# Order of two steps in an RWKV-7 recurrence: sums of squares and features ahead of the state's products and update

## The chip, the cores and the metric

One core of a Trainium2 chip. The metric is the device time of one execution in microseconds (us), the median of several executions. The profile is one further execution taken by the hardware profiler.

## The reference, cut to what matters

The kernel computes a stack of transformer blocks on 256 tokens of width 1024. The change lies in one part of it, the bidirectional RWKV-7 time mixing. For each direction and each of 16 heads of width 64 the reference runs

```
state = state * w_t + (state @ a_t) outer b_t + v_t outer k_t
y_t   = state @ r_t
```

over the tokens (`a_t` is -kk, `b_t` is kk times the learning rate), forward and backward, followed by a group norm, a bonus term and a gate. Everything after it (attention, mixtures of experts, MLPs) is untouched.

## The kernel before

The recurrence works on 8 chunks. A chunk here is a pair of heads (128 channels on the partitions) over all 256 tokens and both directions z. The tokens are two blocks of 128; the state S0 carries the first block's result to the second. Within a chunk the triangular systems are solved by five levels of products: TensorE makes W (`level_w`, L937), ScalarE copies it to `Wb`, TensorE makes the two products XY (`level_xy`, L950 and L955), and VectorE adds them (`level`).

The work is a software pipeline written out by hand. One loop `for s in range(-2, C + 2)` stands on each of TensorE (`pe`), ScalarE (`act`), VectorE (`dve`) and, in a shorter form, GpSimd (`pool`). In pass s the engines work on chunk e = s+2 (norms and decay inputs), f = s+1 (features), c = s (levels), p = s-1 (solve with the state) and g = s-2 (group norm, gate), each only where the number lies in 0..7 (`on_e`, `on_f`, `on_c`, `on_p`, `on_g`). Every engine goes through its list in order; semaphores (`ev(...)`) tie them together.

Steps that the text names:
- features of chunk f on VectorE: four products of 512 columns giving `ar`, `bt`, `kt`; at the end `rw_feat` is raised (L2334). GpSimd, TensorE and ScalarE (its square for e) wait on it.
- sums of squares sm0, sm1 of chunk f on TensorE: 64 products of 64x64 from `ar` and `bt` (L1060). ScalarE copies half of each to `Ast`, VectorE multiplies the other half by a mask (`x0`) and then gives the bank back (L2349).
- S, the state's increment, on TensorE (L1032), and the update of S0 on VectorE (four small products, L2072).
- Z1, products of `ar` with S0 on TensorE (L1047), added to `Zv` by VectorE.
- P1, R1, U1: the solve of the second token block (L964, L974, L984).
- BK, transposes of `bt` and `kt` (L1076); rb (L1086); kk (L1092), the norms' sums of chunk e; var (L1065), the variance of chunk g.
- `ada_blocks(1)`: a step on VectorE of 128x2048 elements that belongs to the adaptive-norm products of another part and is woven into the recurrence. It reads a ring tile loaded by DMA.

All these results of TensorE lie in PSUM. The group "rw" has four banks. `RW_SLOT` lists all tiles in the order in which a pass claims them; `RWN` numbers them through all passes, and tile number m uses bank m mod 4. `claim` lets TensorE wait until tile m-4 has been given back:

```
def claim(g, m, it=None, per=0):
    ...
    elif m >= n:
        pe.wait_ge(free(g, m), m // n)
    return tile(g, m)
```

Of the kernel before, what the change touches and what calls it, by code (L numbers as in the profile page):

```python
# [27 lines left out]
P = 128  # L28
S = 256
# [271 lines left out]
def _plan(name, lo, hi=0, align=False, flip=0, out=0):  # L301
# [8 lines left out]

RW_SLOT = (("P0", 1), ("mean", 2), ("R0", 1), ("U0", 1), ("Zv", 0), ("S", 1), ("V", -1), ("Z1", 1), ("sm0", -1), ("sm1", -1),
           ("var", 2), ("P1", 1), ("BK", -1), ("R1", 1), ("rb0", -1), ("rb1", -1), ("kk", -2), ("U1", 1), ("wa0", -2), ("wa1", -2),
           ("n60", -1), ("n61", -1), ("y", 1), ("bn", -1), ("g", 2), ("ka0", -1), ("ka1", -1), ("kr0", -1), ("kr1", -1))
RWN = {}
# [132 lines left out]
def build(nc, d, out_d):  # L449
    ctx = ExitStack()  # L450
    with ctx:
# [100 lines left out]
        ar = [work(1024).rearrange("p (i n) -> p i n", i=2) for _ in range(3)]  # L552
# [6 lines left out]
        Zv = [work(512) for _ in range(2)]  # L559
# [4 lines left out]
        S0 = work(256).rearrange("p (z n) -> p z n", z=2)  # L564
        ys, sq = work(512), work(512)
        fac = [work(2) for _ in range(3)]
        HALF = (slice(0, 64), slice(64, 128))
# [11 lines left out]
        def ev(name):  # L579
            if name not in named:  # L580
                named[name] = sem(name)
            return named[name]
# [225 lines left out]
        def _(pe):  # L808
            mm = nc.tensor.matmul
# [104 lines left out]
            def rwkv():  # L914
# [3 lines left out]
                def cl(k, i):  # L918
                    return claim("rw", RWN[k, i])

                def fin(ins):
                    ins.then_inc(tile_ready["rw"], 1)

                def gone(k, i):
                    pe.wait_ge(free("rw", RWN[k, i]), RWN[k, i] // 4 + 1)
# [62 lines left out]
                for s in range(-2, C + 2):  # L988
                    e, f, c, p, g = s + 2, s + 1, s, s - 1, s - 2
                    on_e, on_f, on_c, on_p, on_g = e < C, 0 <= f < C, 0 <= c < C, 0 <= p < C, 0 <= g < C  # L990
# [20 lines left out]
                    if on_c:  # L1011
# [3 lines left out]
                        t = cl("Zv", c)  # L1015
                        for z in (0, 1):
                            for j in (0, 1):
                                for h in (0, 1):
                                    a = z * 256 + j * P + 64 * h
                                    last = mm(t[:, a:a + 64], Aak[:, h, z, j, :], Vt[c % 3][:, j, 64 * h:64 * h + 64], start=True, stop=True)  # L1020
# [3 lines left out]
                    if on_p:  # L1024
                        gone("U0", p)
                        gone("BK", p)
                        t = cl("S", p)
                        for z in (0, 1):
                            for i in (0, 1):
                                for h in (0, 1):  # L1030
                                    r = HALF[h]
                                    last = mm(t[r, 64 * z:64 * z + 64], BK[p % 2][:, z, i, r], Vt[p % 3][:, z, r] if i else Uu[:, 0, z, r],  # L1032
                                              start=i == 0, stop=i == 1, skip_group_check=True)
                        fin(last)
                    if on_f:
                        t = cl("V", f)
                        for j in range(2):
                            last = nc.tensor.transpose(t[:, j * P:(j + 1) * P], vT[:, f, j * P:(j + 1) * P], ident)
                        fin(last)
                    if on_c:  # L1040
                        level_w(c, 3)
                    if on_p:
                        gone("S", p)
                        t = cl("Z1", p)
                        for z in (0, 1):
                            a = z * 256 + (1 - z) * P
                            last = mm(t[:, z * P:z * P + P], ar[p % 3][:, 0, a:a + P], S0[:, z, :], start=True, stop=True)  # L1047
                        fin(last)
                    if on_f:
                        pe.wait_ge(ev("rw_feat"), f + 1)  # L1050
                        t = [cl(f"sm{h}", f) for h in (0, 1)]
                        for i in (0, 1):
                            for z in (0, 1):
                                for j in (0, 1):
                                    for b in (0, 1):
                                        a = slice(z * 256 + j * P + 64 * b, z * 256 + j * P + 64 * b + 64)
                                        o = 256 * i + (2 * z + j) * 64
                                        for h in (0, 1):
                                            x_, y_ = ar[f % 3][HALF[h], 0, a], bt[HALF[h], a]
                                            last = mm(t[h][HALF[b], o:o + 64], y_ if i else x_, x_ if i else y_, start=True, stop=True)  # L1060
                                            if (i, z, j, b) == (1, 1, 1, 1):
                                                fin(last)
                    if on_g:
                        pe.wait_ge(ev("rw_sq"), g + 1)
                        fin(mm(cl("var", g), blk64, sq, start=True, stop=True))  # L1065
# [5 lines left out]
                    if on_f:  # L1071
                        t = cl("BK", f)
                        for z in (0, 1):
                            for i in (0, 1):
                                a = z * 256 + z * P
                                last = nc.tensor.transpose(t[:, (2 * z + i) * P:(2 * z + i + 1) * P], (kt if i else bt)[:, a:a + P], ident)  # L1076
# [5 lines left out]
                    if on_f:  # L1082
                        t = [cl(f"rb{h}", f) for h in (0, 1)]
                        for q in range(4):
                            for h in (0, 1):
                                last = mm(t[h][:, q * P:(q + 1) * P], bt[HALF[h], q * P:(q + 1) * P], ar[f % 3][HALF[h], 1, q * P:(q + 1) * P],  # L1086
                                          start=True, stop=True)
# [9 lines left out]
                    if on_e:  # L1097
                        for z in (0, 1):
                            t = cl(f"wa{z}", e)
                            for i in range(2):  # L1100
                                last = mm(t[:, i * S:(i + 1) * S], lora2[HALF[z], i * D + e * P:i * D + (e + 1) * P], th[HALF[z], i, :],
                                          start=True, stop=True)
                            fin(last)
                    if on_f:
                        t = [cl(f"n6{h}", f) for h in (0, 1)]
                        for z in (0, 1):
                            for j in (0, 1):
                                a = z * 256 + j * P
                                for h in (0, 1):
                                    last = mm(t[h][HALF[z], 64 * j:64 * j + 64], bt[HALF[h], a + 64 * z:a + 64 * z + 64],  # L1110
                                              ar[f % 3][HALF[h], 0, a + 64 - 64 * z:a + 128 - 64 * z], start=True, stop=True)
# [4 lines left out]
                    if on_p:  # L1116
# [3 lines left out]
                        t = cl("y", p)  # L1120
                        for z in (0, 1):
                            for ji in (0, 1):
                                j = z if ji == 0 else 1 - z
                                a = z * 256 + j * P
# [6 lines left out]
                                for h, r in enumerate(HALF):  # L1131
                                    last = mm(t[r, a:a + P], Vt[p % 3][:, j, r], Ark[p % 2][:, h, z, j, :], start=False, stop=True,
                                              skip_group_check=True)
# [4 lines left out]
                    if on_g:  # L1138
                        t = cl("g", g)
                        for z in (0, 1):  # L1140
                            last = mm(t[:, z * S:z * S + S], lora2[:, (2 + z) * D + g * P:(2 + z) * D + (g + 1) * P], th[:, 2 + z, :],
                                      start=True, stop=True)
# [3 lines left out]
                    if on_f:  # L1146
                        for i, k in ((0, "ka"), (1, "kr")):
                            t = [cl(f"{k}{h}", f) for h in (0, 1)]
                            for q in range(4):
                                for h in (0, 1):  # L1150
                                    last = mm(t[h][:, q * P:(q + 1) * P], kt[HALF[h], q * P:(q + 1) * P],
                                              ar[f % 3][HALF[h], i, q * P:(q + 1) * P], start=True, stop=True)
# [904 lines left out]
        def _(dve):  # L2057
            chain, own = sem("dve_chain"), [0]
            v = nc.vector
            MUL, ADD, SUB = ALU.mult, ALU.add, ALU.subtract  # L2060
# [10 lines left out]
            def ts(out, a, s1, s2, o1, o2=ALU.bypass):  # L2071
                return v.tensor_scalar(out, a, s1, s2, o1, o2)  # L2072
# [177 lines left out]
            def rwkv():  # L2250
# [3 lines left out]
                def got(k, i):  # L2254
                    ready(dve, "rw", RWN[k, i])
                    return tile("rw", RWN[k, i])

                def let(ins, k, i):
                    ins.then_inc(free("rw", RWN[k, i]), 1)
# [25 lines left out]
                for s in range(-2, C + 2):  # L2285
                    e, f, c, p, g = s + 2, s + 1, s, s - 1, s - 2
                    on_e, on_f, on_c, on_p, on_g = e < C, 0 <= f < C, 0 <= c < C, 0 <= p < C, 0 <= g < C
                    if s == -1:
                        modulation("ada1")
                    if on_f:  # L2290
# [4 lines left out]
                        for j in range(2):  # L2295
                            o, i_ = (a[:, S:2 * S][:, j * P:(j + 1) * P] for a in (cum, ea))
                            last = v.tensor_tensor_scan(o[:, ::-1], ones, i_[:, ::-1], 0.0, MUL, SUB)
# [19 lines left out]
                        K(stt(two(cum), both(kkx), float(2 ** 20), two(ea[:, 512:1024]), MUL, MUL))  # L2317
                    if on_c:
                        level(c, 2)
                    if on_p:  # L2320
                        t = got("S", p)
                        for z in (0, 1):
                            for r in HALF:
                                last = ts(S0[r, z, r], t[r, 64 * z:64 * z + 64], fac[p % 3][r, z:z + 1], None, MUL)
                        let(last, "S", p)
                    if on_f:
                        dve.wait_ge(ev("rw_E"), f + 1)
                        a_ = ar[f % 3]
# [2 lines left out]
                    if on_f:  # L2331
                        tt(bt, cum, e3, MUL)
                        K(tt(kt, km, e3, MUL))
                        dve.sem_inc(ev("rw_feat"), 1)  # L2334
                    if on_p:
                        a = Zv[p % 2][:, P:3 * P]
                        let(tt(a, got("Z1", p)[:, 0:S], a, ADD), "Z1", p)
                        ada_blocks(1)
                    if on_c:
                        level(c, 3)  # L2340
                    if on_f:
                        x0 = rmask("x0").rearrange("p (z t) -> p z t", z=2)[:, :, None, :].to_broadcast([P, 2, 2, 64])
                        X = XY[f % 3][:, :, 0, :]
                        for h in (0, 1):
                            dve.wait_ge(ev("rw_A"), 2 * f + h + 1)
                            t = got(f"sm{h}", f)[:, 256:512].rearrange("p (z j t) -> p z j t", z=2, j=2)
                            last = tt(X[:, :, h * P:(h + 1) * P].rearrange("p z (j t) -> p z j t", j=2), t, x0, MUL)
# [622 lines left out]
```

## Time and profile before

| | us |
|---|---|
| median of 3 runs | 3048.99 |
| lowest, highest | 3048.26, 3053.26 |
| profiled execution, its own time | 3056.66 |
| its span (first to last instruction) | 3054.9 |

The span is what the profile's times run over; the profiled execution's own time is 1.76 us more. TensorE is busy for 93% of the span, VectorE 68%, ScalarE 53%. The recurrence runs from about 160 us to 500 us of it; one full pass takes 40 us.

### The profile page before, as it was taken

How to read it: one execution, taken by the hardware profiler on the slowest of the kernel's cores; microseconds unless marked ns; L12 is line 12 of the kernel's file. 1: busy time of each engine (PE TensorE's matmuls, PEld its weight loads, DVE VectorE, ACT ScalarE, POOL GpSimd, SP SyncE). 2: the span in 40 equal slices, each digit the busy share in tenths (PEclk: the TensorE clock that was granted, in tenths of full speed). 3: DMA queues.
4: the chain of work that ended last, by engine and by line, in shares of the span. 5: the costliest groups of instructions: out<-in, count | busy, mean ns of one | idle time of the engine just before them, and what ended most of it. 6: DMA issues, size and time to landing. Idle time of an engine off the chain costs nothing.

```text
span 3054.9 us, 54359 instructions
## 1 busy us (share of the span) xinstructions
PE 2840.3 (93%) x22781; PEld 2570.3 (84%) x22781; DVE 2068.8 (68%) x2604; ACT 1610.3 (53%) x2268; POOL 155.4 (5%) x164
## 2 busy tenths in 40 slices
PE   6878888899998999899999999999899979999999
PEld 5867767777777999877877889998899869998999
DVE  7767775699996656589998565454545775556554
ACT  3444432488884444378887454444444724445443
POOL 0033340000000020100000000000000000000000
PEclk8989997899998999899999999999999989999999
DMA  8501113399995736179998414544255304543353
GB/s 323 210 2 44 57 57 135 132 351 358 357 351 200 276 124 262 42 274 353 354 357 327 152 42 152 180 164 166 97 181 188 141 14 167 185 159 138 122 182 124
DMA packets 78262, 572.85 MB, mean 188 GB/s; under 512 B 8802, under 2 KB 8802, under 8 KB 9186
## 3 DMA queue, kind: packets, MB, share of 16 engines
q1 hardware_dynamic: 76752, 558.93, 49.4%
q10 hardware_dynamic: 1298, 10.90, 0.9%
q8 instruction: 157, 2.57, 0.3%
q14 instruction: 55, 0.45, 0.0%
HBM read 568.74 MB, written 1.05 MB: 187 GB/s over the span
## 4 chain that ended last, share of the span: by engine, by line
PE 82%; DVE 12%; ACT 3%; DMA 2%; issue 1%; POOL 0%; DVEq 0%; SPq 0%; ACTq 0%; PEldq 0%
PE ps L1295 13%; PE ps L1219 12%; PE ps L832 9%; PE ps L833 9%; PE ps L834 9%; PE ps L1316 7%; DVE arena L2075 4%; DVE arena L2069 2%; DMA ring<-in_stream 2%; DVE wl L2069 1%; PE ps L855 1%; PE ps L854 1%; PE ps L853 1%; PE ps L1389 1%; DVE hl L2069 1%
## 5 line engine op out<-in xcount | busy, mean ns | idle before, releaser
L2069 DVE TENSOR_TENSOR wl<-ring,wh 128x1024 fp32r<-128x1024 f32 (+1 forms) x560 | 937.9, 1695 | 489.1 <-ACT wh L1509 483.1
L1509 ACT ACTIVATE wh<-ring 128x1024 fp32r<-128x1024 f32 (+1 forms) x560 | 789.0, 1431 | 515.1 <-PE ps L834 310.3
L832 PE MATMUL ps<-hh,wh 128*128 128x256 f32 x2464 | 715.8, 291 | 50.5 <-DVE hl L2069 40.7
L833 PE MATMUL ps<-hh,wl 128*128 128x256 f32 x2464 | 705.2, 286 | 0.0
L834 PE MATMUL ps<-hl,wh 128*128 128x256 f32 x2464 | 704.9, 286 | 0.0
L832 PEld LDWEIGHTS ps<-hh,wh 128*128 128x128 f32 x2464 | 481.1, 195 | 61.6 <-issue 42.6
L833 PEld LDWEIGHTS ps<-hh,wl 128*128 128x128 f32 x2464 | 481.4, 195 | 3.1 <-issue 2.9
L834 PEld LDWEIGHTS ps<-hl,wh 128*128 128x128 f32 x2464 | 481.2, 195 | 0.0
L1219 PE MATMUL ps<-hidh,wh 128*128 128x256 f32 x1024 | 290.2, 283 | 0.3 <-DVE hidl L2069 0.3
L1219 PE MATMUL ps<-hidh,wl 128*128 128x256 f32 x1024 | 289.8, 283 | 0.0
L1219 PE MATMUL ps<-hidl,wh 128*128 128x256 f32 x1024 | 289.8, 283 | 0.0
L1509 ACT ACTIVATE arena<-ps 128x512 f32<-128x512 f32 (+3 forms) x158 | 86.9, 550 | 305.3 <-PE ps L834 195.0
L1506 ACT ACTIVATE arena<-arena 128x256 f32<-128x256 f32 (+7 forms) x420 | 205.9, 495 | 67.7 <-DVE arena L2626 16.3
L1295 PE MATMUL ps<-wh,parts 128*128 128x512 f32 x656 | 225.6, 405 | 1.2 <-DVE parts L2069 1.2
L1295 PE MATMUL ps<-hh,parts 128*128 128x512 f32 x624 | 211.6, 400 | 0.0
L1219 PEld LDWEIGHTS ps<-hidh,wh 128*128 128x128 f32 x1024 | 196.6, 192 | 1.1 <-DVE hidl L2069 1.1
L1219 PEld LDWEIGHTS ps<-hidh,wl 128*128 128x128 f32 x1024 | 196.6, 192 | 0.0
L1219 PEld LDWEIGHTS ps<-hidl,wh 128*128 128x128 f32 x1024 | 196.6, 192 | 0.0
L2069 DVE TENSOR_TENSOR hl<-ring,hh 128x1024 fp32r<-128x1024 f32 x160 | 189.6, 1219 | 5.0 <-ACT hh L1509 4.1
L1509 ACT ACTIVATE hh<-ring 128x1024 fp32r<-128x1024 f32 x160 | 168.0, 1061 | 35.6 <-PE ps L1295 29.3
L2075 DVE SCALAR_TENSOR_TENSOR arena<-ps,arena 128x512 f32<-128x512 f32 (+4 forms) x134 | 81.2, 618 | 121.1 <-PE ps L834 81.7
L2069 DVE TENSOR_TENSOR arena<-ps,arena 128x512 f32<-128x512 f32 (+2 forms) x145 | 86.3, 621 | 90.3 <-PE ps L955 39.8
(260 smaller groups left out, 4668.4 us busy)
## 6 DMA issues: line engine op xcount, KB each, us to landing
ring<-in_stream SPq DMA_DIRECT2D x532, 1024.0 KB, 4.9
arena<-in_wcmp ACTq DMA_DIRECT2D x2, 2048.0 KB, 10.4
arena<-in_lora ACTq DMA_DIRECT2D x1, 2048.0 KB, 9.8
arena<-in_atm ACTq DMA_DIRECT2D x1, 1762.0 KB, 7.6
x<-in_xT ACTq DMA_DIRECT2D x1, 1024.0 KB
out<-x SPq DMA_DIRECT2D x1, 1024.0 KB, 3.8
arena<-in_rwm ACTq DMA_DIRECT2D x1, 736.0 KB, 12.8
cols<-in_cols ACTq DMA_DIRECT2D x1, 715.0 KB
```

What stands on the lines that cost most here:

```text
L832: mm(out, w[0], h[0], start=first, stop=False)
L833: mm(out, w[1], h[0], start=False, stop=False)
L834: return mm(out, w[0], h[1], start=False, stop=last)
L853: mm(o, a[0], W[0][:, k, :], start=k == 0, stop=False)
L854: mm(o, a[1], W[0][:, k, :], start=False, stop=False)
L1219: last = mm(o, W[a][:, f, c * P:(c + 1) * P], H[b][:, f, :], start=False, stop=False, skip_group_check=True)
L1295: last = mm(t, h[a][:, k, :], w[c][:, k, :], start=part == 0 and k == 0 and n == 0, stop=part == 1 and k == 3 and n == 2)
L1316: last = mm(t[n], h[a][:, f, :], w[c][:, f, 512 * n:512 * n + 512], start=e % INNER == 0 and f == 0 and j == 0, stop=e % INNER == INNER - ...
L1506: return nc.scalar.activation(out, in_, f, scale=scale, bias=bias, **k)
L1509: return nc.scalar.activation(out, in_, ACT.Copy)
L2069: return v.tensor_tensor(out, a, b, op)
L2075: return v.scalar_tensor_tensor(out, a, s, b, o1, o2)
```

## The change

On TensorE the sums of squares of the next chunk f are issued ahead of Z1. On VectorE the features of chunk f are computed ahead of the update of S0. `RW_SLOT` follows TensorE's new order, so that Z1 stands behind sm0 and sm1 in the turn of the four banks. No instruction is added or removed.

```
-RW_SLOT = (("P0", 1), ("mean", 2), ("R0", 1), ("U0", 1), ("Zv", 0), ("S", 1), ("V", -1), ("Z1", 1), ("sm0", -1), ("sm1", -1),
+RW_SLOT = (("P0", 1), ("mean", 2), ("R0", 1), ("U0", 1), ("Zv", 0), ("S", 1), ("V", -1), ("sm0", -1), ("sm1", -1), ("Z1", 1),
            ("var", 2), ("P1", 1), ("BK", -1), ("R1", 1), ...
 TensorE
                     if on_c:
                         level_w(c, 3)
-                    if on_p:
-                        gone("S", p)
-                        t = cl("Z1", p)
-                        for z in (0, 1): ... mm(..., S0[:, z, :], ...)
-                        fin(last)
                     if on_f:
                         pe.wait_ge(ev("rw_feat"), f + 1)
                         t = [cl(f"sm{h}", f) for h in (0, 1)]
                         ...
+                    if on_p:
+                        gone("S", p)
+                        t = cl("Z1", p)
+                        ...
                     if on_g:
                         pe.wait_ge(ev("rw_sq"), g + 1)
 VectorE
                     if on_c:
                         level(c, 2)
-                    if on_p:
-                        t = got("S", p)
-                        for z in (0, 1):
-                            for r in HALF:
-                                last = ts(S0[r, z, r], t[r, 64 * z:64 * z + 64], fac[p % 3][r, z:z + 1], None, MUL)
-                        let(last, "S", p)
                     if on_f:
                         dve.wait_ge(ev("rw_E"), f + 1)
                         ... (ar, bt, kt)
                         dve.sem_inc(ev("rw_feat"), 1)
+                    if on_p:
+                        t = got("S", p)
+                        ... (the same four products)
+                        let(last, "S", p)
                     if on_p:
                         a = Zv[p % 2][:, P:3 * P]
                         let(tt(a, got("Z1", p)[:, 0:S], a, ADD), "Z1", p)
                         ada_blocks(1)
```

## Rows read from the trace of the kernel before

**Rows 1.** Windows view, three stretches; then busy time and count of each engine, PEclk, DMA

```profile
301.60:341.60 40.00, 33.88 (x728) 28.00 (x726) 31.89 (x54) 16.78 (x43) 15.43 (x14) 1.00 0.15 55
341.60:383.30 41.70, 35.58 (x731) 28.97 (x727) 32.38 (x54) 16.88 (x43) 15.39 (x14) 0.96 0.15 53
...
344.00:346.00 2.00, 1.87 (x65) 1.76 (x65) 1.85 (x3) 0.00 (x0) 1.85 (x2) 0.56 0.00 0
```

**Rows 2.** Waits view of the stretch 301.6 to 341.6: total, times, longest

```profile
PE ps L1060 <- DVEq L2334: 1.8, 1, 1.8
...
PE ps L937 <- DVE arena L2069: 1.2, 1, 1.2
...
PE ps L1101 <- DVE arena L2069: 1.2, 1, 1.2
...
PE ps L1151 <- ACT spare L1509: 1.1, 1, 1.1
PE ps L1076 <- DVEq L2349: 0.9, 1, 0.9
```

**Rows 3.** Timeline of TensorE, pass s=3: start, length, what, [idle before]

```profile
301.59 0.71 PE L1047 MATMUL ps<-spare,arena 128*128 128x128 f32 x4
304.07 0.69 PE L1060 MATMUL ps<-under,arena 64*64 64x64 f32 x32 [1.77 <-DVEq L2334]
...
305.17 1.12 PE L1065 MATMUL ps<-spare,mats 128*128 128x512 f32 x2
306.22 0.68 PE L950 MATMUL ps<-under,arena 64*64 64x64 f32 x16
...
308.14 0.40 PE L964 MATMUL ps<-spare,arena 64*64 64x64 f32 x8
309.49 0.66 PE L1076 MATMUL ps<-mats,under 128*128 128x128 f32 x4 [0.95 <-DVEq L2349]
...
312.30 0.70 PE L1092 MATMUL ps<-under,mats 128*128 128x256 f32 x2
```

**Rows 4.** Timeline of VectorE in the same pass

```profile
300.25 1.18 DVE L2072 TENSOR_SCALAR spare<-ps,arena 64x64 f32<-64x64 f32 x4
301.46 0.69 DVE L2069 TENSOR_TENSOR arena<-arena,under 128x512 f32<-128x512 f32 x1
...
302.68 1.28 DVE L2069 TENSOR_TENSOR under<-under 128x512 f32<-128x512 f32 x2
304.11 0.42 DVE L2069 TENSOR_TENSOR spare<-ps,spare 128x256 f32<-128x256 f32 x1 [0.15 <-DVE under L2069]
304.45 3.07 DVE L2075 SCALAR_TENSOR_TENSOR ring<-ring,small 128x2048 f32<-128x2048 f32 x1
307.45 0.68 DVE L2069 TENSOR_TENSOR arena<-ps,arena 128x512 f32<-128x512 f32 x1
308.35 1.02 DVE L2069 TENSOR_TENSOR arena<-ps,arena 128x512 f32<-128x512 f32 x2 [0.23 <-PE ps L955]
309.60 0.42 DVE L2069 TENSOR_TENSOR arena<-ps,arena 128x256 f32<-128x256 f32 x1 [0.23 <-DVE arena L2069]
...
319.12 2.83 DVE L2075 SCALAR_TENSOR_TENSOR ring<-ring,small 128x2048 f32<-128x2048 f32 x1
```

**Rows 5.** Timeline of ScalarE in the same pass

```profile
308.58 0.55 ACT L1509 ACTIVATE spare<-ps 64x128 f32<-64x128 f32 x2 [2.64 <-PE ps L964]
...
311.55 0.59 ACT L1509 ACTIVATE arena<-ps 128x512 f32<-128x512 f32 x1
```

**Rows 6.** Timeline of TensorE in passes s=1 and s=4

```profile
229.68 0.66 PE L1076 MATMUL ps<-mats,under 128*128 128x128 f32 x4
...
344.13 1.07 PE L1060 MATMUL ps<-under,arena 64*64 64x64 f32 x32 [1.78 <-DVEq L2334]
...
345.98 1.94 PE L1065 MATMUL ps<-spare,mats 128*128 128x512 f32 x2
```

**Rows 7.** Timeline of VectorE in pass s=1

```profile
228.79 1.78 DVE L2069 TENSOR_TENSOR arena<-ps,arena 128x512 f32<-128x512 f32 x3
```

More of the change, by code:

```diff
@@ L1041, in rwkv @@
                         level_w(c, 3)
-                    if on_p:
-                        gone("S", p)
-                        t = cl("Z1", p)
-                        for z in (0, 1):
-                            a = z * 256 + (1 - z) * P
-                            last = mm(t[:, z * P:z * P + P], ar[p % 3][:, 0, a:a + P], S0[:, z, :], start=True, stop=True)
-                        fin(last)
                     if on_f:
@@ L1062, in rwkv @@
                                                 fin(last)
+                    if on_p:
+                        gone("S", p)
+                        t = cl("Z1", p)
+                        for z in (0, 1):
+                            a = z * 256 + (1 - z) * P
+                            last = mm(t[:, z * P:z * P + P], ar[p % 3][:, 0, a:a + P], S0[:, z, :], start=True, stop=True)
+                        fin(last)
                     if on_g:
@@ L2319, in rwkv @@
                         level(c, 2)
-                    if on_p:
-                        t = got("S", p)
-                        for z in (0, 1):
-                            for r in HALF:
-                                last = ts(S0[r, z, r], t[r, 64 * z:64 * z + 64], fac[p % 3][r, z:z + 1], None, MUL)
-                        let(last, "S", p)
                     if on_f:
@@ L2334, in rwkv @@
                         dve.sem_inc(ev("rw_feat"), 1)
+                    if on_p:
+                        t = got("S", p)
+                        for z in (0, 1):
+                            for r in HALF:
+                                last = ts(S0[r, z, r], t[r, 64 * z:64 * z + 64], fac[p % 3][r, z:z + 1], None, MUL)
+                        let(last, "S", p)
                     if on_p:
```

## The prediction

> **What bounds the kernel now.** I read the windows view first, one stretch for each pass of the recurrence's stage loop. A full pass takes 40.0 us and TensorE (PE) is busy for 33.9 of them, VectorE (DVE) for 31.9, ScalarE (ACT) for 16.8 [rows 1]. Neither PE nor DVE is full, so the pass is a closed loop of waits with PE on it most of the time. The waits view of a pass names the idle pieces of PE: 1.8 us in front of the sums of squares (L1060) until DVE has marked the features, 0.9 us in front of the transposes BK (L1076) until a PSUM bank is given back by DVE (L2349), and 1.1 to 1.2 us each at L1101, L1151 and L937 [rows 2]. The change touches only the first two. The timelines of the three engines over the middle of the pass s=3 then give the order in which each step frees the next [rows 3, 4, 5].
>
> **Where the edit bears.** Both `on_p` and `on_f` hold in the passes s=1 to 6, so six passes change. In the others one of the two blocks is absent and the order of instructions and banks is as before.
>
> **DVE, first part.** Before, the update of S0 (four products, L2072) starts at 300.25 and the features start at 301.46, so the update takes 1.21 us of DVE. The features end at 302.68 + 1.28 = 303.96, and PE's first product of sums starts at 304.07, which is 0.11 after [rows 3, 4]. Nothing but the update stands between the end of level 2 on DVE and the features; no idle is recorded at 301.46. With the features first they start at 300.25, end at 302.75, and PE may start at 302.86. The update of S0 starts 0.15 after their end (the gap that stands at 304.11 today), at 302.90, and ends at 304.08 [rows 4].
>
> **PE, first part.** The sums run 302.86 to 303.96 (304.07 to 305.17 today). The products with the state (Z1) now come behind them and wait for S0: 304.08 + 0.1 = 304.18. They take 0.71, with the next work following about 0.1 before the modelled end, at 304.80. The variance product (var) takes 1.05 (305.17 to 306.22), so level 3's products start at 305.85 instead of 306.22, and end 1.92 later (306.22 to 308.14), at 307.77 [rows 3]. Up to here PE has gained 0.37 us. That is all that the 1.21 us earlier start is worth, because Z1 was work that filled part of the wait before.
>
> **DVE, second part: the loss.** The addition of Z1 was ready to go at 304.11. Now it waits for PE's Z1, which ends at 304.89, and starts at 304.95, 0.84 later. Behind it on DVE stands an ada block of 3.0 us (304.45 to 307.45), and behind that level 3's two additions and the first product of the sums (L2345 and after), all in order [rows 4]. So level 3 starts at 308.29, its second half at 308.90, the first product of sm0 at 309.51 and ends at 309.93. Today that product ends at 308.35 + 1.02 = 309.37. The transfer of 0.84 shrinks to 0.56 as today's second addition waits 0.23 for PE [rows 4].
>
> **The bank turn.** The tiles of the recurrence go round four PSUM banks in the order of RW_SLOT, and a tile waits until the one four places earlier is given back. Today P1 follows Z1 (given back at 304.53) and BK follows sm0. In the new order V, sm0, sm1, Z1, var, P1, BK, R1, the tile P1 follows sm0 and BK follows sm1. P1's products (L964) today start at 308.14 without idle and BK waits until 309.49 [rows 3]. Now P1 itself has to wait for sm0: 309.93 + 0.12 = 310.05 (the 0.12 is today's 309.37 to 309.49). BK waits for the second product of sums, 309.60 + 0.42 today and 0.56 later now: 310.58, and PE starts BK at 310.70, which is 1.21 us later than before. PE's gain of 0.37 is lost in this wait.
>
> **ACT, behind P1.** ACT copies P1's result from 308.58, 0.44 after P1 started on PE, and then goes through seven instructions in order without a recorded idle time: two copies, logarithm, exponential, square, level 4's two copies, and last the copy of BK, which ends at 311.55 + 0.59 = 312.14 [rows 5]. That is 3.56 us. P1 at 310.05 puts the copies at 310.49 and the end of BK's copy at 314.05. The tile kk (L1092) follows BK in the bank turn, and starts at 312.30 today as soon as rb's products are through [rows 3]. PE would now reach it at 310.70 + 2.81 = 313.51, but BK's bank comes at 314.05 + 0.12 = 314.17. So the pass is 1.87 us late at kk: 1.21 from the sums and 0.66 from ACT.
>
> **Does a later wait take it up?** The next waits of PE are L1101 (1.2 us, until DVE's product of rb), L1151 (1.1 us, until ACT's copy of y) and L937 (1.2 us, until DVE's level 1 addition) [rows 2]. Each is behind work that PE itself released a little earlier (level 4's products, g, ka), so all of it moves with PE. The ada block earlier or later moves no transfer that anyone waits for: DVE records no idle on its ring tile [rows 4]. GpSimd gets the features 1.21 earlier, and nobody waits for it here. So I carry the 1.87 whole into the next pass; what follows the recurrence starts later by the sum.
>
> **Each pass.** s=2, 3 and 5 are as computed: 3 x 1.87 = 5.61. In s=1 there is no var, mean or logarithm, P1 follows V (free) and BK follows sm0. The three DVE operations from 228.79 end at 230.57; the shift of Z1's addition is 0.83 by the same steps, so sm0 comes at 231.40 and BK at 231.52 instead of 229.68: +1.84 [rows 6, 7]. In s=4 PE ran 344 to 346 at a granted clock of 0.56 [rows 1], the lower of its two levels (1.2 against 2.4 GHz), right after the 1.8 us idle. The sums took 1.85 there (344.13 to 345.98) against 1.10, and the var product 1.94 against 1.12 [rows 3, 6]. PE is then late for level 3 by itself and DVE waits for it, so part of the loss is hidden: if the slow stretch keeps its place in time, the same steps give +0.7, and if it moves with the work +1.4. I take 1.1. s=6 is like s=4 but has no kk (no head pair is left), so only the delay of BK counts, 0 to 0.6: I take 0.3. Sum: 1.84 + 5.61 + 1.1 + 0.3 = 8.85 us. Not shown by any row is whether S0's update slows down when GpSimd works beside it. The nearest rows are the two ada blocks of a pass, 3.07 and 2.83 us [rows 4], 8% apart, and 8% of 1.21 is 0.1 us a pass; at the other end nothing. I take nothing, since these products are small; the bound adds 0.6 in all.
>
> The profiled execution took 3056.66 us with a span of 3054.9, 7.7 above the median of 3048.99. The sum is made of differences inside a pass, so I put it on the median: 3048.99 + 8.85 = 3057.8. On the profile the span would be 3063.8.
>
> The Trainium skill, Perfetto Trace Analysis, section Optimization Strategy, says that the same gap coming back on the engine that should be full can mean that there is no buffer for the next tile. The trace has such a gap at BK [rows 2]; by that rule the fault sits in the bank turn and the edit, which puts P1 into it too, makes it larger. It changes no number above.
>
> **Rivals.**
> 1. The forecast, +8.85: chance 0.58.
> 2. ACT's chain does not hold up kk, and the slow-clock passes hide the whole loss: s=1 gives 1.84, the three full passes 1.21 each, together +5.5, so 3054.5. For it: 0.66 of my 1.87 hangs on seven ACT operations being packed exactly as today. Against it: they show no idle [rows 5]. It decides if they take under 2.9 us. Chance 0.15.
> 3. The clock. PE today fell to the lower level after an idle of 1.8 us in s=4 and not in s=3 [rows 1, 3]. The new wait before P1 is 310.05 - 307.77 = 2.3 us, with shorter ones following. One such stretch cost 0.75 on the sums and 0.82 on var, 1.6 us, which is also what the pass s=4 is longer than s=3 [rows 1, 3, 6]. If each of the three full passes gets one more: 8.85 + 4.8 = 13.7, so 3062.7. Chance 0.18. The Trainium skill, TensorE: Matmul & The Clock Gate, "What's actually happening", says that throttled is the default and activity releases it; the stretch at 0.56 behind an idle piece agrees. By that rule a longer idle piece makes this rival likelier.
> 4. Faster: the wait for sm0 before P1 does not come last. Then PE keeps 0.37 and today's 0.95 before BK goes as well, 1.32 a pass in five passes: -6.6, so 3042.4. It needs sm0 given back by 307.8, 2.2 us ahead of what DVE's order gives, so about as if the ada block of 3.0 us were not in front of it. Nothing in the rows shortens that block. Chance 0.05.
> 5. Taken up: the delay vanishes in the later waits of the pass and the time is the same, 3049. Chance 0.04.
>
> **How the numbers follow.** About 0.2% (6.1 us) is what a measurement of this kernel tells from no change. Case 1 spreads by about 3 us (the clock's places, the bounds above, the spread of the three runs), so some of it falls under 6.1. Slower: 0.50 of case 1, 0.18 of case 3, 0.03 of case 2, 0.71. Same: the rest of 1 and 2 and case 5, 0.24. Faster 0.05. The range from 3052 to 3064 takes in cases 1 to 3.
>
> **What would show it.** In a full pass: L1060 starts 1.2 us earlier after level 3's L937; L1047 behind it with little idle; a new idle piece of about 2 us before L964, put down to L2349; L1076's wait reduced to some 0.3; a new idle piece of 0.6 before L1092 put down to ACT; the pass 41.9 us long instead of 40.0. I am wrong if L964 starts without idle, if the passes s=2, 3 and 5 stay at 40.0, or if PE's granted clock falls in other passes.

## The result, and the profile after

| | us |
|---|---|
| before, median of 18 runs | 3051.95 (3047.39 to 3061.05) |
| changed, median of 18 runs | 3060.43 (3051.99 to 3065.30) |
| ratio of changed to before | 1.0024, 95% interval 1.0017 to 1.0030 |
| span of the profiled execution, before / changed | 3054.9 / 3063.4 |

The changed kernel is slower by 0.24%, 7.3 us of 3052 (5 to 9 by the interval). The ratio compares the two sets of runs. It is not the quotient of the two medians, which lie a little further apart, 8.5 us.

First the windows view: one pass of the kernel before (s=2), then the changed kernel. Its stretches are the passes s=2 to 5. Each stretch runs from the start of the transposes V (L1038) to the next one. Columns as in [rows 1].

```profile
260.09:300.14 40.05, 33.93 (x731) 28.03 (x727) 31.95 (x54) 16.83 (x42) 15.44 (x14) 1.00 0.16 54
...
258.08:299.16 41.08, 34.03 (x730) 28.06 (x726) 31.27 (x54) 16.70 (x42) 15.38 (x14) 1.00 0.15 53
299.16:341.74 42.58, 35.51 (x731) 29.18 (x727) 30.80 (x54) 16.82 (x42) 15.35 (x14) 0.96 0.14 52
341.74:383.78 42.04, 35.50 (x731) 29.34 (x727) 31.28 (x54) 16.70 (x42) 15.38 (x14) 0.96 0.16 52
383.78:427.26 43.48, 36.96 (x730) 30.45 (x726) 30.77 (x54) 16.99 (x42) 15.29 (x14) 0.92 0.14 51
```

The changed kernel's first pass here, at a granted clock of 1.00, takes 41.08 us where the kernel before takes 40.05. The other three contain stretches at the lower level of TensorE's clock (0.96 and 0.92 in the mean) and take 0.96 to 2.4 us more. A pass "undisturbed" is from here on one with 1.00.

The timeline of TensorE in the pass s=3, answering to [rows 3]. In the changed kernel L1053 are the sums of squares, L1061 is Z1.

```profile
301.87 0.69 PE L1053 MATMUL ps<-under,arena 64*64 64x64 f32 x32 [1.19 <-DVEq L2328]
...
303.24 0.68 PE L1061 MATMUL ps<-spare,arena 128*128 128x128 f32 x4 [0.21 <-DVE spare L2072]
303.76 1.02 PE L1065 MATMUL ps<-spare,mats 128*128 128x512 f32 x2
304.71 0.68 PE L950 MATMUL ps<-under,arena 64*64 64x64 f32 x16
...
308.43 0.45 PE L964 MATMUL ps<-spare,arena 64*64 64x64 f32 x8 [1.63 <-DVEq L2349]
308.99 0.66 PE L1076 MATMUL ps<-mats,under 128*128 128x128 f32 x4
...
312.41 0.67 PE L1092 MATMUL ps<-under,mats 128*128 128x256 f32 x2 [0.54 <-ACT arena L1509]
```

The sums wait 1.19 instead of 1.77 us, Z1 waits 0.21 for S0, and then the two new idle pieces stand: 1.63 us before P1 (L964) until VectorE's L2349 gives back sm0's bank, and 0.54 before kk (L1092) until ScalarE. No idle time stands before BK (L1076) any more, but it still starts only when its bank comes: at 308.99, 0.12 after the second product of the sums ends on VectorE (308.45 + 0.42).

The timeline of VectorE over the same pass, answering to [rows 4]:

```profile
299.27 0.68 DVE L2069 TENSOR_TENSOR arena<-arena,under 128x512 f32<-128x512 f32 x1
...
301.92 1.18 DVE L2072 TENSOR_SCALAR spare<-ps,arena 64x64 f32<-64x64 f32 x4 [0.16 <-DVE under L2069]
303.96 0.42 DVE L2069 TENSOR_TENSOR spare<-ps,spare 128x256 f32<-128x256 f32 x1 [0.86 <-PE ps L1061]
304.30 2.39 DVE L2075 SCALAR_TENSOR_TENSOR ring<-ring,small 128x2048 f32<-128x2048 f32 x1
306.62 1.61 DVE L2069 TENSOR_TENSOR arena<-ps,arena 128x512 f32<-128x512 f32 x3
308.45 0.42 DVE L2069 TENSOR_TENSOR arena<-ps,arena 128x256 f32<-128x256 f32 x1 [0.23 <-DVE arena L2069]
```

The features follow level 2 at once (299.27) and the update of S0 follows them (301.92). Then VectorE is idle for 0.86 us until Z1 comes. The addition of Z1 (303.96), the ada block (304.30, 2.39 us), level 3 and the first product of the sums (from 306.62) follow in order. ScalarE, answering to [rows 5]:

```profile
308.91 0.56 ACT L1509 ACTIVATE spare<-ps 64x128 f32<-64x128 f32 x2 [5.17 <-PE ps L964]
...
311.67 0.60 ACT L1509 ACTIVATE arena<-ps 128x512 f32<-128x512 f32 x1
```

P1 starts at 308.43, ScalarE's copies of it at 308.91, and the copy of BK ends at 312.27; kk starts at 312.41.

### The profile page after: what moved, and what is told of

Read it like the earlier page. It is cut to its first block, busy times and chain, and to the rows that moved or that the text cites. A ratio compares the mean times of both kernels' runs of the same rounds, so it can differ in the third digit from the quotient of the medians.

```text
span 3063.4 us, 54359 instructions
## 1 busy us (share of the span) xinstructions
PE 2840.1 (93%) x22781; PEld 2569.1 (84%) x22781; DVE 2063.3 (67%) x2604; ACT 1609.8 (53%) x2268; POOL 155.6 (5%) x164
## 3 DMA queue, kind: packets, MB, share of 16 engines
q8 instruction: 157, 2.57, 0.3%
## 4 chain that ended last, share of the span: by engine, by line
PE 79%; DVE 13%; ACT 3%; DMA 2%; issue 1%; POOL 0%; DVEq 0%; SPq 0%; ACTq 0%; PEldq 0%
PE ps L1295 13%; PE ps L1219 12%; PE ps L832 9%; PE ps L834 9%; PE ps L833 9%; PE ps L1316 6%; DVE arena L2075 4%; DMA ring<-in_stream 2%; DVE arena L2069 2%; DVE wl L2069 2%; DVE hl L2069 1%; PE ps L855 1%; PE ps L854 1%; PE ps L853 1%; PE ps L1389 1%
## 5 line engine op out<-in xcount | busy, mean ns | idle before, releaser
L1295 PEld LDWEIGHTS ps<-wh,parts 128*128 128x128 f32 x656 | 123.4, 188 | 28.3 <-issue 2.0
```

The source lines that it names most:

```text
L1295: last = mm(t, h[a][:, k, :], w[c][:, k, :], start=part == 0 and k == 0 and n == 0, stop=part == 1 and k == 3 and n == 2)
```

## The experiments

Each ratio is to the kernel before, with its 95% interval. The pass is the undisturbed one, 40.05 before and 41.08 changed. There is no e5. Undisturbed passes were read in several places of each profile and agree to 0.02 us.

| kernel | ratio | pass, us |
|---|---|---|
| e1, VectorE half alone | 1.0016 (1.0007 to 1.0026) | 40.74 |
| e2, TensorE half alone | 1.0046 (1.0034 to 1.0058) | 42.31 |
| e3, changed + banks freed first | 0.9967 (0.9955 to 0.9980) | 39.26 |
| e4, before + banks freed ahead of level 3 | 0.9988 (0.9979 to 0.9998) | 39.80 |
| e6, changed + pb behind two masks | 1.0027 (1.0016 to 1.0038) | 41.09 |
| e7, changed + copy of BK earlier | 1.0018 (1.0007 to 1.0029) | 40.54 |
| e8, combination | 0.9973 (0.9961 to 0.9985) | 38.73 |
| e9, changed + pb beside the ada block | 1.0042 (1.0029 to 1.0056) | none undisturbed |
| e10, e3 again | 0.9965 (0.9954 to 0.9977) | 39.26 |
| e11, e8 again | 0.9970 (0.9956 to 0.9983) | 38.71 |

### Each half alone

**e1.** On VectorE the update of S0 behind the features; `RW_SLOT` and TensorE as before.

> VectorE half alone: the features of f ahead of the update of S0; TensorE's order and the bank turn as before. My account of waits: in a full pass S0 is ready at 304.08 on the clock of pass s=3 of before, so TensorE's Z1 starts at 304.18 instead of 301.59 and the sums at 304.8 instead of 304.07; everything behind keeps that, +0.73 us a pass, with P1 still free of a wait. Six passes: about +4 us. If instead the changed kernel lost its time by the clock alone and not by waits, this one is within 2 us of before.

Timeline of TensorE in e1, pass s=2, and the window of that pass:

```profile
259.55 0.71 PE L1047 MATMUL ps<-spare,arena 128*128 128x128 f32 x4 [2.46 <-DVE spare L2072]
...
265.60 0.66 PE L1076 MATMUL ps<-mats,under 128*128 128x128 f32 x4 [0.95 <-DVEq L2349]
...
255.56:296.30 40.74, 33.94 (x731) 28.04 (x727) 31.39 (x54) 16.84 (x42) 14.51 (x14) 1.00 0.15 54
```

Z1 now waits 2.46 us for S0, BK's 0.95 stays, and the pass is 0.69 longer (0.73 expected). Ratio 1.0016, +4.9 us.

**e2.** On TensorE the sums ahead of Z1, with the new `RW_SLOT`; on VectorE the update of S0 ahead of the features, as before.

> TensorE half alone, with its bank turn: the sums ahead of Z1; VectorE's order as before. My account of waits: the sums start at 304.07 as before, Z1 ends at 305.9, the addition of Z1 starts at about 305.95 instead of 304.11, the ada block (2.4 us, as in the changed kernel) and level 3 follow, sm0's bank comes at 310.25 and P1 starts at 310.4 instead of 308.14; kk at about 314.3 instead of 312.30. +2.0 us a pass, so +10 to +12 us in all, the slowest of all. Rival (the bank turn is harmless, only the late features matter): within 0.2% of before.

The same views of e2:

```profile
264.71 0.69 PE L1053 MATMUL ps<-under,arena 64*64 64x64 f32 x32 [2.42 <-DVEq L2334]
...
271.25 0.45 PE L964 MATMUL ps<-spare,arena 64*64 64x64 f32 x8 [1.87 <-DVEq L2349]
...
275.24 0.67 PE L1092 MATMUL ps<-under,mats 128*128 128x256 f32 x2 [0.53 <-ACT spare L1509]
...
260.78:303.09 42.31, 33.99 (x731) 28.06 (x727) 31.54 (x54) 16.72 (x42) 15.39 (x14) 1.00 0.15 52
```

P1 waits 1.87 us for sm0's bank and kk 0.53, on top of the sums' 2.42. The pass is 2.26 us longer (2.0 expected) and the whole 14 us (10 to 12 expected). Each half alone loses by a wait of its own; together they lose 1.03 a pass, more than the VectorE half and less than the TensorE half.

### Taking the bank out of the wait

**e3.** The changed kernel, VectorE:

```
+                    if on_f:
+                        x0 = ... ; X = XY[f % 3][:, :, 0, :]
+                        for h in (0, 1): ... (products with x0, free sm0 and sm1)
                     if on_p:
                         a = Zv[p % 2][:, P:3 * P]
                         let(tt(a, got("Z1", p)[:, 0:S], a, ADD), "Z1", p)
                         ada_blocks(1)
                     if on_c:
                         level(c, 3)
                     if on_f:
-                        (the same products)
                         X4 = ...
```

> The changed kernel, with VectorE's two products that free the banks of sm0 and sm1 moved up, ahead of the addition of Z1 and the ada block. TensorE's order and the bank turn stay as in the changed kernel. If the bank of sm0 behind the ada block is what costs the time, P1 (L964) starts without idle, BK too, level 3 on VectorE ends later by some 0.7 us, kk comes 1.7 us earlier in a pass than in the changed kernel and about 0.6 earlier than before: -8 us against the changed kernel, -3 us against before. If the loss is in Z1 and the update of S0 themselves, or in the clock, it stays at +6 to +9 us against before.

Timeline of TensorE in e3, pass s=2, and its window:

```profile
262.02 0.69 PE L1053 MATMUL ps<-under,arena 64*64 64x64 f32 x32 [1.19 <-DVEq L2328]
...
266.78 0.40 PE L964 MATMUL ps<-spare,arena 64*64 64x64 f32 x8
267.11 0.66 PE L1076 MATMUL ps<-mats,under 128*128 128x128 f32 x4
268.31 1.10 PE L937 MATMUL ps<-arena 64*64 64x64 f32 x26 [0.55 <-DVE arena L2069]
...
259.31:298.57 39.26, 33.92 (x730) 28.09 (x726) 31.79 (x54) 16.70 (x42) 15.44 (x14) 1.00 0.16 56
```

No row shows an idle time before L964, L1076 or L1092 any more; what is left is 0.55 before level 4's L937, for level 3's addition. The pass is 1.82 shorter than the changed kernel's and 0.79 shorter than before, and the kernel is 10 us faster than before. TensorE's new order and the new bank turn are unchanged in e3, so they alone don't cost the time. VectorE's place for the two products that free the banks, behind the addition of Z1, the ada block and level 3, does.

Only a third of the 10 us comes from waits. Against the kernel before, e3 gains 0.79 in each of s=2 to 5 and 0.77 in s=6, and loses 0.34 in s=1 and 0.28 in s=0: 3.3 us in all, which is the 3 us expected. The medians of e3 and of its repetition e10 lie 7.8 and 8.1 us below before, so by them too the whole gained more than the waits. What part of the rest the clock can explain is said further down.

**e4.** The kernel before, with the same two products between the ada block and level 3.

> The kernel before, with VectorE's two products that free sm0 and sm1 moved ahead of level 3's additions (behind the ada block). The wait of 0.95 us before BK (L1076) goes to about 0.3. My account says that this gives almost nothing, 0 to -0.2 us a pass, because kk (L1092) then waits for ScalarE's chain behind P1 (the copy of BK ends at 312.14 as before). Rival 2 of the prediction, that this chain does not hold up kk: then -0.4 to -0.6 us a pass, -3 us.

```profile
270.19 1.10 PE L937 MATMUL ps<-arena 64*64 64x64 f32 x26 [0.39 <-DVE arena L2069]
...
272.76 0.67 PE L1092 MATMUL ps<-under,mats 128*128 128x256 f32 x2
...
272.02 0.60 ACT L1509 ACTIVATE spare<-ps 128x512 f32<-128x512 f32 x1
...
260.82:300.62 39.80, 34.10 (x730) 28.16 (x727) 32.02 (x54) 16.73 (x42) 15.29 (x14) 1.00 0.16 55
```

That is the timeline of TensorE in e4 (s=2), ScalarE's copy of BK and the pass. The pass gains 0.25 (0 to 0.2 expected, 0.4 to 0.6 by rival 2), so most of the removed 0.95 comes back. One part is the new 0.39 before L937, which waits for VectorE's level 3. Another is ScalarE's chain: kk (L1092) starts 0.14 after the copy of BK ends (0.16 in the kernel before), and 1.30 after rb instead of 1.09, so this part is 0.2 us. The ratio, 0.9988, is -3.7 us, more than 0.25 a pass can give (1.5 in six), with an interval that reaches down to -0.6.

### ScalarE's chain

**e7.** The changed kernel, ScalarE: `let(copy(BK...))` ahead of `level(c, 4)` instead of behind it.

> The changed kernel, with ScalarE's copy of BK ahead of its two copies of level 4 instead of behind them. The idle piece of 0.54 us before kk (L1092) goes, since BK's bank comes back 0.5 us earlier; level 4's copies come 0.5 us later and still in time. By my account of ScalarE's chain an undisturbed pass takes 40.5 to 40.6 us instead of 41.08, about 2.5 us less in all. If this chain does not set the end of the pass (rival 2), nothing changes.

```profile
314.15 0.67 PE L1092 MATMUL ps<-under,mats 128*128 128x256 f32 x2
...
301.46:342.00 40.54, 34.02 (x730) 28.06 (x726) 31.27 (x54) 16.70 (x42) 15.38 (x14) 1.00 0.15 54
```

In this undisturbed pass of e7 (s=3) the idle time before kk is gone and the pass is 0.54 shorter than the changed kernel's. The share that the prediction gave to ScalarE (0.66) is real and 0.54 in size. The ratio of 1.0018 against 1.0024 (1.8 us less, 2.5 expected) points the same way, but the intervals overlap.

### The term that was too large

**e6.** The changed kernel, GpSimd's product pb behind its two level-5 masks (`later(c, 5)`).

> The changed kernel, with GpSimd's product pb (L2897, 128x512) issued behind its two level-5 masks instead of ahead of them, so that it runs beside VectorE's ada block again, as it did in the kernel before. In the profiles so far the first ada block of a pass took 3.07 us where pb ran beside it and 2.39 where only masks did; this is the term that my sum had 0.7 us too large. If pb beside it is the reason, the block goes back to about 3.0 us here, P1 (L964) starts some 0.6 us later in a pass and an undisturbed pass takes 41.6 to 41.8 us instead of 41.08. If the duration hangs on something else in the new order, it stays at 2.4 and the pass at 41.1.

Timeline of VectorE (the ada block) and of GpSimd (pb) in e6, pass s=2, and the window of the pass:

```profile
264.75 2.38 DVE L2075 SCALAR_TENSOR_TENSOR ring<-ring,small 128x2048 f32<-128x2048 f32 x1
...
263.72 1.26 POOL L2897 TENSOR_TENSOR under<-under 128x512 f32<-128x512 f32 x1
...
259.61:300.70 41.09, 34.03 (x730) 28.07 (x727) 31.27 (x54) 16.70 (x42) 15.38 (x14) 1.00 0.14 53
```

pb ran until 264.98 and did overlap the block's start, and the block still took 2.38. The theory "pb beside it" fell. What differs is how much of the GpSimd instruction was left. GpSimd in the kernel before, whose block started at 304.45 [rows 4]:

```profile
304.10 1.28 POOL L2897 TENSOR_TENSOR under<-under 128x512 f32<-128x512 f32 x1 [13.52 <-DVEq L2334]
...
305.33 2.78 POOL L2897 TENSOR_TENSOR arena<-under,arena 128x256 f32<-128x256 f32 x1
```

and in the changed kernel, whose block started at 304.30:

```profile
301.90 1.27 POOL L2897 TENSOR_TENSOR under<-under 128x512 f32<-128x512 f32 x1 [12.29 <-DVEq L2328]
...
303.82 0.72 POOL L2897 TENSOR_TENSOR arena<-under,arena 128x256 f32<-128x256 f32 x1
...
304.51 2.77 POOL L2897 TENSOR_TENSOR arena<-under,arena 128x256 f32<-128x256 f32 x1
```

Before, 0.88 us of pb was left until the next GpSimd start at 305.33, and the block took 3.07. Changed, 0.21 was left and it took 2.39. In e6 0.19 was left, 2.38. The GpSimd mask behind took 2.77 to 2.78 each time, against 0.72 for its like. It ends 0.59 us after VectorE's block (308.11 and 307.52 before, 307.28 and 306.69 changed), so it seems to have waited for the block and then done its own work.

**e9.** The changed kernel, pb behind the first half of GpSimd's Y product instead.

> The changed kernel with GpSimd's product pb moved behind the first half of its Y product, so that pb (1.27 us) should start just before VectorE's ada block does. In all profiles so far the first ada block took 2.35 us plus what was left of the GpSimd instruction in flight when it started, less about 0.16 (3.07 with 0.88 left, 2.39 with 0.21 left; in e6 pb had 0.19 left and the block took 2.38). Theory: VectorE's block waits for the instruction in flight. Here pb starts at about 304.2 on the clock of pass s=3, the block at 304.30, so it should take 3.2 to 3.4 us, P1 should come 0.9 us later and an undisturbed pass take 41.9 to 42.1 us. If only the kind of neighbour mattered or the new order itself, the block stays at 2.4 and the pass at 41.1.

Timelines of e9: the ada block and pb in the pass s=3, and P1 in the pass s=2.

```profile
308.82 3.34 DVE L2075 SCALAR_TENSOR_TENSOR ring<-ring,small 128x2048 f32<-128x2048 f32 x1
...
308.75 1.27 POOL L2897 TENSOR_TENSOR under<-under 128x512 f32<-128x512 f32 x1
...
270.93 0.45 PE L964 MATMUL ps<-spare,arena 64*64 64x64 f32 x8 [2.59 <-DVEq L2349]
```

pb starts 0.07 ahead of the block, and the block takes 3.34 (3.2 to 3.4 expected); P1 waits 2.59 instead of 1.63. No pass is undisturbed (42.7 to 44.1), so the pass itself can't be compared with the 42.0 expected. The whole is 1.0042.

### What is fastest

**e8.** e3, with `ada_blocks(1)` moved from behind Z1's addition to behind `solved_r(p, 1)`, and e7's edit.

> The changed kernel with the two products that free sm0 and sm1 first (as in the third experiment), the ada block moved from behind the addition of Z1 to behind the addition for R1 (VectorE waits 2.8 us for TensorE there), and ScalarE's copy of BK ahead of level 4's copies. By my account the 0.55 us that TensorE still waits for level 3's addition go away and nothing new comes last: 38.7 us a pass instead of 39.26, 12 to 13 us less than before in all. If the ada block in its new place holds up level 4 or the product of rb, a pass stays at 39.3 or gets longer.

The pass is 38.73, as expected, but the whole is only 8 us faster by the ratio of 0.9973, where 12 to 13 were expected. So e3 and e8 were run once more on one chip as e10 and e11.

> The kernel of the third experiment (the two products that free sm0 and sm1 first) once more, beside the combination of the eighth, to tell the two apart on one chip: 0.997 of before, undisturbed passes of 39.26 us.

> The kernel of the eighth experiment once more. Its undisturbed pass was 0.53 us shorter than that of the third (38.73 against 39.26), which by waits alone is 2.7 us less, a ratio of 0.999 to the third; yet its first ratio to before was 0.9973 against 0.9967. If the waits decide, it comes out ahead by 1 to 3 us here; if the stretches at the low clock take it back, the two are equal.

```profile
258.46:297.17 38.71, 33.75 (x730) 27.95 (x726) 31.78 (x54) 16.70 (x42) 15.39 (x14) 1.00 0.16 57
```

That is an undisturbed pass of e11 (s=2). The waits did what was expected (38.71), and so did those of e10 (39.26). The ratios, 0.9965 and 0.9970, don't tell the two apart, and the medians point the other way: 3043.82 for e10 and 3041.52 for e11, 2.3 us less, with executions of each spread over 8 us. Whether e11 is ahead by the expected 1 to 3 us stays open. By their four ratios the kernels are 8 to 11 us faster than before. That the low clock takes back e8's 0.5 us a pass is not shown.

### The clock, two more profiles

> The changed kernel once more, for its profile. The waits of TensorE must be the same to 0.1 us (1.63 before P1, 0.54 before kk, an undisturbed pass 41.08). If the stretches at the low granted clock are set by the waits, they stand in the same passes; if they depend on when the execution starts, they stand elsewhere and their number differs.

> The kernel before once more, for its profile. The waits as in the first profile (1.78 before the sums, 0.95 before BK, an undisturbed pass 40.05). If the stretches at the low clock follow from the order of work alone, they stand in the same passes (s=4 and s=6); if not, elsewhere.

The changed kernel again: the waits are the same to 0.01 us, an undisturbed pass is 41.09. The passes from s=1 on (mark to mark) took 37.01, 42.01, 41.09, 42.57, 42.03, where the first profile had 38.47, 41.08, 42.58, 42.04, 43.48; the span was 3051.0 instead of 3063.4. The kernel before again: 36.03, 41.60, 41.64, 40.04, 41.61 instead of 37.54, 40.05, 40.05, 41.64, 40.04, span 3047.3 instead of 3054.9. In e6, whose waits are those of the changed kernel, no pass from s=1 to 5 had a slow stretch. So the slow stretches stand elsewhere in each execution of the same program, and one profile's span says little about a change of 6 us.

The mean granted clock of every single execution says more than the profiles do. It is 0.9609 over the 28 executions of the changed kernel and of e6, which has the same waits. It is 0.9617 over the 74 of the kernel before that ran beside e1 to e11, and 0.9633 over the 15 of e3 and e10. The differences to before, 0.0008 less and 0.0016 more, are just clear of their 95% intervals (0.0007 and 0.0008 either way). Among the executions of one and the same kernel, 0.001 less clock goes with 1.7 us more. An estimate from these numbers is that the clock costs the changed kernel 1.4 us and gives e3 2.8 us. All kernels with a longer pass than before have 0.9608 together (65 executions), all with a shorter one 0.9627 (47). So longer waits go together with more time at the low level. That the waits bring it about is likely, but no run shows it.

## Why the prediction was right

3060.4 was measured where 3057.8 was forecast (range 3052 to 3064), slower by more than 0.2%. The step sums, against undisturbed passes:

- **The start of the sums, 1.21 earlier.** The features follow level 2 at once and the sums wait 1.19 instead of 1.77. Counted from the start of the sums, Z1 was forecast at 1.32 and came at 1.37, var at 1.94 and 1.89, level 3's products at 2.99 and 2.84. Counted from V, the addition of Z1 came 0.83 later than before (0.84 forecast).
- **The bank turn.** P1 waits for sm0 and BK follows the second product: right. e3 shows it by taking the wait away. P1's wait was 1.63 us instead of 2.28. BK's, forecast at some 0.3, is too small for the view to print: BK starts 0.56 after P1, and 0.33 after it in e3, so about 0.2.
- **The mis-sized term** is "an ada block of 3.0 us". In the new order it held VectorE for 2.32 (304.30 to 306.62), 0.68 less, because it meets a GpSimd instruction with 0.21 left and not 0.88. I had taken the duration over from [rows 4] without asking what was in it. e6 and e9 show the cause. With it, counted from V, P1 came 1.27 later than before instead of 1.91, BK 0.48 instead of 1.21 and kk 1.09 instead of 1.87.
- **The term put at nothing**, a slower update of S0 beside GpSimd, was nothing: 1.18 us with pb beside it (from 301.90) and 1.18 before, without.
- **ScalarE's chain** took 3.36 instead of 3.56 (level 4's two copies 0.64 instead of 0.84) and held kk for 0.54 instead of 0.66; e7 confirms that it is the chain.
- **Each pass.** Forecast +1.87 (+1.1 in s=4), measured +1.03 in s=2 to 5. With profiles without a slow stretch in these places, s=1 gives 37.02 (e6) against 36.03 (the second profile of before), +0.99 (1.84 forecast). In s=6, from V to Z1 of the next pass, it is 38.99 against 38.52, +0.47 (0.3 forecast). Sum: 0.99 + 4 x 1.03 + 0.47 = 5.6 us where 8.85 was forecast. The discount in s=4 rested on a slow stretch that keeps its place, and the second profile of before has none there.
- **Nothing is taken up later.** The waits at L1101, L1151 and L937 are 1.16, 1.06 and 1.17 to 1.18 in both kernels. Rival 5 is out.
- **Rival 2** is out: the chain does hold kk. **Rival 4** is out as forecast, but e3 is that rival made real: with sm0 given back ahead of the ada block the new order is 10 us faster than before. A pass gains 0.79 there and not 1.32, since level 3 comes later and TensorE waits 0.55 for it.
- **Rival 3, the clock.** 7.3 us measured less 5.6 from waits leaves 1.7, within the interval (5 to 9); by the medians 2.9 are left. The changed kernel's profiles had four, three and (as e6) no slow stretches in the passes s=2 to 5, those of before one and three, which decides nothing. The granted clocks of all executions do: the estimate of 1.4 us fits what is left. So this rival is true in part, at about a third of its 4.8 us.
- **A sign of being wrong came true.** The prediction called itself wrong if the granted clock fell in other passes. It did: in the first profiles it fell in s=1, 4 and 6 before, and in s=1, 3, 4, 5 and 6 changed. The sign was badly chosen, since the second profile of the unchanged kernel has its stretches in s=2, 3 and 5. The waits forecast stand at their places in all three profiles with the changed kernel's waits, whatever the clock did.

So the forecast (+8.85 against +7.3 by the ratio) landed close partly by luck, because two errors offset: waits too large by 3.3 us, and 1.7 us that don't come from waits, for which it had no term. The median of before, over more runs, is also 3 us above the one that the forecast started from, which brings the forecast 3057.8 below the 3060.4 measured.

## What to carry to other kernels

When an order is changed on an engine whose outputs go round a few banks, write down the new turn and ask for each tile who gives back the bank it now gets, and what stands ahead of that release on the other engine. Move the releasing operation with the tile: the same reorder cost 7 us without that step and gained 10 us with it (by waits alone it cost 5.6 and gained 3.3). A duration taken from a trace can contain a wait, so look at what shares a resource with the instruction at its start before using it in another order.

## What the runs showed of the hardware

The ada block (VectorE, two inputs and the output in SBUF) and a GpSimd instruction seem to exclude each other for their whole length. The 128x2048 block takes 2.35 us when it starts first. It took 2.38, 2.39, 3.07 and 3.34 us with 0.19, 0.21, 0.88 and 1.15 us left of the GpSimd instruction in flight, which is 2.35 plus what is left, less about 0.16. The sum also fits e2 (2.63 us with 0.44 left) and e11 (2.57 with 0.38), from which it was not made. The 128x256 GpSimd mask took 2.77 us behind the block instead of 0.72, both engines booked as busy. The update of S0, whose input lies in PSUM, took 1.18 us with and without GpSimd beside it. The Trainium skill, SBUF — State Buffer, section "SBUF: two separate sides", says that VectorE and GpSimd share a port pair as an exclusive lock. A VectorE instruction with two SBUF inputs and a GpSimd instruction that reads SBUF contend for it, the first one holds it for the whole instruction, and the loser blocks fully. These rows agree.

TensorE's slow stretches (at the lower of its levels, 1.2 GHz) cost 0.9 to 1.6 us each in a pass and stood in other passes in each execution of the same program. Over all executions the kernels with longer waits had the lower mean granted clock (0.9608 against 0.9617 for before and 0.9627 for those with shorter waits).
